# Routing chunk by chunk inside the last output unit, first expert's tokens by slot-matrix products, gates by pair in the last round

## Chip, cores and metric

The kernel runs on one core of one Trainium2 chip. The metric is the device time of one execution in microseconds (us), lower is better. The core's engines are named as the profile names them: PE (matrix products; PEld its weight loads), DVE (vector), ACT (scalar), POOL (GpSimd) and SP, which here only issues DMAs.

## The reference, cut to what matters

One decoder block over 512 tokens of width 1024: a mixer of four retention heads and four dilated attention heads, an output projection added to the input, then a mixture of experts in which each token goes to 4 of 32 experts, and a last RMSNorm. The part around the change:

```python
x = x + hybrid_mixer(rms_norm(x, norm_mix_g[l]), w_in[l], w_out[l], pos)
x = x + moe_ffn(rms_norm(x, norm_ffn_g[l]), ...)
# moe_ffn:
logits = (ht @ w_router + b_router).astype(jnp.float32)
top_val, top_idx = lax.top_k(logits, TOP_K)                     # 4 of 32
gates = jax.nn.softmax(top_val, axis=-1).astype(h.dtype)
...                                                             # tokens sorted by expert, blocks of 128 rows
gu = xb @ w_gu + b_gu                                           # 128 x 1024 by 1024 x 2048
act = min(x_glu, 7) * sigmoid(1.702 * x_glu) * (clip(x_lin, -7, 7) + 1)
y = act @ w_dn + b_dn                                           # 128 x 1024 by 1024 x 1024
out.at[rows_tok].add(y * rows_gate[:, None])
```

## The kernel before

All weights come in units of 1 MB (128 partitions x 2048 numbers). Units 0 to 13 are the input projection, 14 to 17 the output projection (`U_OUT`), and from 18 on (`U_MOE`) each expert has 8 gate and up units and 4 down units. Each unit is loaded by SP into a raw slot, split by ACT into a rounded high part (`hi(n)`, line 693) and by DVE into the remainder (`lo(n)`, line 992), and PE makes three products with it (activation high and low by weight high, activation high by weight low): 12 products of 512 columns a unit. There are four split slots, so `hi(n)` waits until PE has used unit n-4, and six raw slots, so SP loads unit n once `lo(n-6)` is done. Every engine has its program written out by hand, and semaphores carry the order between them. An engine that waits holds up all that stands behind it in its own program.

The 512 tokens are four chunks of 128 (`c` = 0..3). In the last output unit (`out_project(U_OUT + 3, c)`) PE finishes the second half of each chunk's output, DVE adds it to the residual (`residual(1)`, line 1155), POOL multiplies the chunk by the norm's gain (`hn`, line 557), ACT sums its squares (line 805), and PE transposes the halves (line 1603) and multiplies them with the router (line 1613). When all four chunks are there, DVE makes the root, the logits, the four choices and a 0/1 mask for all of them at once (lines 1166 to 1193), PE turns the masks into places in the experts' lists (1638 to 1642), and DVE compares them with slot numbers (`has`, line 1198). PE makes from that the row numbers of expert 0 and 1 (1651), and POOL gathers the rows of expert 0 from memory (line 595), after which PE transposes them (`tokens`, 1663) and ACT and DVE split them. `first_gate_up` then runs expert 0's eight gate and up units (1685, 1687, 1693).

For the other experts a table in memory is used. POOL stores it with 16 indirect DMAs (`store_entries`, line 611), reads it back (`tab`, line 635), and copies a column as the index of each gather. In the main loop, round i runs the gate and up units of expert i+1 (`gate_up`, lines 1722 to 1727), `tokens(2, i)`, which transposes the rows gathered for expert i+2, and the down units of expert i. POOL in a round: two bias rows spread over the partitions (lines 526 and 534), the gather for expert i+3, the scatter of expert i (601, 605). After 30 rounds a tail handles the last two experts, and the biases of the down projection are added as one product of the gates by pair (`gate4`) and all 32 rows.

Before the loop starts, these things stand behind one another on POOL, in this order: the bias spread of expert 0, the gather for expert 0, four entries, a bias spread, four entries, the gather for expert 1, eight entries, the two bias spreads of expert 1 (which `bias_to_gate(1)` on ACT and then the first unit of the loop on PE wait for), the table, the gather for expert 2. DVE makes the gates by pair (1223 to 1231) and the list of overflowing experts (1282 to 1294) before the loop, and ACT waits for that list before `hi(30)`.

Of the kernel before, what the change touches and what calls it, by code (L numbers as in the profile page):

```python
# [25 lines left out]
P = 128  # L26
# [129 lines left out]
def build(nc, x, norm_mix_g, w_in, w_out, norm_ffn_g, w_router, b_router,  # L156
# [77 lines left out]
    pair_gate, o = place(o, "pair_gate", [NC, E])  # L234
    pair_pos, o = place(o, "pair_pos", [NC, E])
    prod, _ = place(area + 70 * K, "prod", [NC * TOPK, E])
    top8, o = place(o, "top8", [NC, 8])
    idx8, o = place(o, "idx8", [NC, 8], U32)
    idxf, o = place(o, "idxf", [NC * TOPK])
# [21 lines left out]
    bias_over, _ = place(area + 12 * K, "bias_over", [2 * D])  # L261
    counts, o = place(area + 20 * K, "counts", [E])
# [11 lines left out]
    x1_at = base + RAW * UNIT * 4 + 2 * SPLIT * UNIT * 4  # L274
    xT0_hi, _ = place(x1_at + 8 * K, "xT0_hi", [KD, P], F32R)
    xT0_lo, _ = place(x1_at + 12 * K, "xT0_lo", [KD, P], F32R)
# [8 lines left out]
    gate4, _ = place(area + 92 * K, "gate4", [NC, 4, E])  # L285
    gateT, o = place(area + 102 * K, "gateT", [S], F32R)
# [35 lines left out]
    pairs_all = sem("pairs_ready")  # L322
    gather_index, scatter_index, order = sem("gather_index"), sem("scatter_index"), sem("gpsimd_order")
    counts_s, total_s = sem("counts_ready"), sem("total_ready")
    sq, var_s, root_s, rstd_s = sem("squares"), sem("variance"), sem("root"), sem("rstd")
# [24 lines left out]
    gate4_s, gate_zero, gate_tr, gateT_hi, gateT_lo = (sem("gates_copied"), sem("gate_rows_cleared"), sem("gates_transposed"),  # L350
# [4 lines left out]
    xg_zero = sem("rows_cleared")  # L355
# [47 lines left out]

    def raw_unit(r, rows):
        return raw_slot(r).rearrange("p (k c) -> p k c", k=rows)
# [15 lines left out]
    with block as block:  # L421
        @block.sync
        def _(sp):
# [19 lines left out]
            def load_bias_rows(e, i):  # L443

                sp.wait_ge(gate_all, i + e)
                sp.dma_start(row_g[0:1, :], b_gate_up[0, bass.ds(i + e, 1), 0:D]).then_inc(bias_in, 16)
                sp.wait_ge(lin_all, i + e)
# [13 lines left out]
            sp.wait_ge(logit_s, 2)  # L461
# [21 lines left out]
            sp.wait_ge(moved, 32 * (E - 2) + 64)  # L483
# [28 lines left out]
        def _(pl):  # L512
# [7 lines left out]
            def spread_gate_bias(e, i=0):  # L520

                pl.wait_ge(bias_in, 16 if e == 0 else i * 32 + 32 * (e + 1))
                if e > 0:
                    pl.wait_ge(bias_gate, i + e)
                    pl.sem_inc(order, 1)
                nc.gpsimd.partition_broadcast(bias_g[:, :], row_g[0:1, :]).then_inc(gate_all, 1)

            def spread_lin_bias(e, i=0):

                pl.wait_ge(bias_in, i * 32 + 32 * (e + 1))  # L530
                if e > 0:
                    pl.wait_ge(bias_lin, i + e)
                    pl.sem_inc(order, 1)
# [25 lines left out]
            pl.wait_ge(logit_s, 2)  # L559
            spread_gate_bias(0)  # L560
            pl.wait_ge(gate_all, 1)
# [1310 lines left out]
```

## Time and profile before

| | us |
|---|---|
| median of 3 runs (1445.2 to 1447.88) | 1445.6 |
| the profiled execution | 1446.0 |
| its span | 1444.2 |
| PE busy | 1387.5 (96%) |
| DVE busy | 1232.4 (85%) |
| ACT busy | 1024.2 (71%) |
| POOL busy | 410.3 (28%) |

Busy time is a share of the whole span. The stretches around the change look different from the average, and a wait counts only if nothing else is late by as much. All instants below are us from the span's start.

### The profile page before, as it was taken

What the parts mean: (1) busy time and instruction counts of PE and PEld (TensorE: products, weight loads), DVE (VectorE), ACT (ScalarE), POOL (GpSimd) and SP (SyncE); (2) the same over time, 40 slices, a digit from 0 to 9 for tenths busy, and PEclk for the clock granted to TensorE, in tenths of its full rate; (3) what the DMA queues carried; (4) which work ended last, traced back from release to release, by engine and by line L of the source; (5) the groups of instructions that cost most, each with busy time, mean ns of one, the idle gap of its engine ahead of it and who ended that gap; (6) DMA issues with size and microseconds to landing.
All of it is one profiled execution on the core that took longest, in us unless ns stands there. A gap on an engine that the chain in (4) does not pass through costs nothing.

```text
span 1444.2 us, 19518 instructions
## 1 busy us (share of the span) xinstructions
PE 1387.5 (96%) x6520; PEld 1153.0 (80%) x6520; DVE 1232.4 (85%) x927; ACT 1024.2 (71%) x750; POOL 410.3 (28%) x231
## 2 busy tenths in 40 slices
PE   6999999877999999999999999999999999999995
PEld 5877888766888888888888888888888888888874
DVE  5534547367999999999999999999999999999986
ACT  5234334465788888888888888888888888888874
POOL 0000001284633333333333333333333333333311
PEclk9999999978999999999999999999999999999998
DMA  8221224456999999999999999999999999999993
GB/s 300 94 82 59 100 76 136 157 211 223 379 396 383 381 384 380 372 374 382 378 382 387 370 382 379 377 382 383 381 376 386 380 386 385 381 385 380 372 338 124
DMA packets 81017, 453.48 MB, mean 314 GB/s; under 512 B 13887, under 2 KB 13903, under 8 KB 32736
## 3 DMA queue, kind: packets, MB, share of 16 engines
q1 hardware_dynamic: 68968, 432.55, 75.6%
q0 software_dynamic: 10304, 18.26, 4.9%
q10 hardware_dynamic: 1720, 2.34, 0.5%
q8 instruction: 16, 0.26, 0.1%
q14 instruction: 9, 0.07, 0.0%
HBM read 447.63 MB, written 22.59 MB: 326 GB/s over the span
## 4 chain that ended last, share of the span: by engine, by line
PE 86%; DMA 4%; DVE 3%; POOL 2%; ACT 2%; issue 2%; ACTq 0%; SPq 0%; DVEq 0%; POOLq 0%
PE ps L1722 14%; PE ps L1727 14%; PE ps L1723 14%; PE ps L1685 8%; PE ps L1687 8%; PE ps L1693 8%; PE ps L1415 4%; PE ps L1423 4%; PE ps L1416 4%; DMA acc_rows<-y,idx_scatter 2%; PE ps L1663 2%; PE ps L1676 2%; ACT whi L693 1%; POOL slot_table L611 1%; POOL idx_scatter L601 1%
## 5 line engine op out<-in xcount | busy, mean ns | idle before, releaser
L992 DVE TENSOR_TENSOR wlo<-raw,whi 128x2048 fp32r<-128x2048 f32 x274 | 648.7, 2390 | 108.0 <-ACT whi L693 107.7
L693 ACT ACTIVATE whi<-raw 128x2048 fp32r<-128x2048 f32 x274 | 520.8, 1914 | 137.2 <-PE ps L1727 91.6
L1722 PE MATMUL ps<-whi,xT_hi 128*128 128x512 f32 x992 | 390.4, 394 | 8.3 <-ACT ps L854 8.3
L1723 PE MATMUL ps<-whi,xT_lo 128*128 128x512 f32 x992 | 387.1, 390 | 0.0
L1727 PE MATMUL ps<-wlo,xT_hi 128*128 128x512 f32 x992 | 266.4, 390 | 0.0
L1722 PEld LDWEIGHTS ps<-whi,xT_hi 128*128 128x128 f32 x992 | 187.0, 189 | 47.0 <-issue 8.7
L1727 PEld LDWEIGHTS ps<-wlo,xT_hi 128*128 128x128 f32 x992 | 186.8, 188 | 38.9
L1723 PEld LDWEIGHTS ps<-whi,xT_lo 128*128 128x128 f32 x992 | 187.1, 189 | 37.9
L1685 PE MATMUL ps<-whi,actT_hi 128*128 128x512 f32 x496 | 195.9, 395 | 0.0
L1687 PE MATMUL ps<-whi,actT_lo 128*128 128x512 f32 x496 | 193.2, 390 | 0.0
L601 POOL COPY idx_scatter<-tab 128x1 uint32 (+1 forms) x31 | 59.0, 1904 | 321.9 <-ACT y L841 321.9
L992 DVE TENSOR_TENSOR wlo<-raw_a,whi 128x2048 fp32r<-128x2048 f32 x64 | 145.9, 2279 | 2.2 <-ACT whi L693 2.0
L992 DVE TENSOR_TENSOR wlo<-raw_b,whi 128x2048 fp32r<-128x2048 f32 x64 | 145.9, 2280 | 1.1 <-ACT whi L693 1.1
L693 ACT ACTIVATE whi<-raw_a 128x2048 fp32r<-128x2048 f32 x64 | 122.8, 1918 | 24.1 <-PE ps L1727 24.1
L693 ACT ACTIVATE whi<-raw_b 128x2048 fp32r<-128x2048 f32 x64 | 122.5, 1915 | 23.9 <-PE ps L1727 23.9
L1693 PE MATMUL ps<-wlo,actT_hi 128*128 128x512 f32 x496 | 132.8, 390 | 0.2 <-DVE wlo L992 0.2
L601 POOL COPY idx_gather<-tab 128x1 uint32 (+1 forms) x31 | 12.6, 406 | 354.7 <-PE ps L1663 353.0
L1693 PEld LDWEIGHTS ps<-wlo,actT_hi 128*128 128x128 f32 x496 | 93.0, 188 | 20.2 <-DVE wlo L992 0.6
L1687 PEld LDWEIGHTS ps<-whi,actT_lo 128*128 128x128 f32 x496 | 93.2, 188 | 18.4
L1685 PEld LDWEIGHTS ps<-whi,actT_hi 128*128 128x128 f32 x496 | 93.2, 188 | 18.4
L534 POOL PARTITION_BROADCAST bias_l<-row_l x32 | 99.5, 3110 | 0.0
L605 POOL DMA_INDIRECT acc_rows<-y,idx_scatter x31 | 87.5, 2824 | 27.4 <-POOL idx_scatter L601 27.4
(229 smaller groups left out, 1648.8 us busy)
## 6 DMA issues: line engine op xcount, KB each, us to landing
raw<-in_w_gate_up SPq DMA_DIRECT2D x130, 1024.0 KB, 8.7
raw<-in_w_down SPq DMA_DIRECT2D x126, 1024.0 KB, 9.4
raw_a<-in_w_gate_up SPq DMA_DIRECT2D x63, 1024.0 KB, 6.8
raw_b<-in_w_gate_up SPq DMA_DIRECT2D x63, 1024.0 KB, 7.3
raw<-in_w_in SPq DMA_DIRECT2D x14, 1024.0 KB, 5.2
raw<-in_w_out SPq DMA_DIRECT2D x4, 1024.0 KB, 5.1
x<-in_x SPq DMA_DIRECT2D x4, 512.0 KB, 8.0
acc_rows<-x SPq DMA_DIRECT2D x4, 512.0 KB, 4.9
```

Source lines behind the costliest of these rows:

```text
L534: nc.gpsimd.partition_broadcast(bias_l[:, :], row_l[0:1, :]).then_inc(lin_all, 1)
L601: return nc.gpsimd.tensor_copy(index[:, 0:1], tab[:, bass.ds(e, 1), 0].bitcast(U32))
L605: pl.indirect_dma_start(out=acc_rows, out_offset=bass.IndirectOffsetOnAxis(ap=idx_scatter[:, 0:1], axis=0), in_=y[:, :], in_offset=None, b ...
L693: nc.scalar.activation(whi_slot(n), raw_slot(slot_of(n)), ACT.Copy).then_inc(hi_done, 1)
L992: nc.vector.tensor_tensor(wlo_slot(n), raw_slot(slot_of(n)), whi_slot(n).bitcast(F32), ALU.subtract).then_inc(lo_done, 1)
L1415: mm(out_ap, x_hi_of(k), w_hi_ap, start=opened and k == 0, stop=False)
L1685: mm(ps[:, bank + half, :], x_hi_t[:, k0 + k, :], w_hi_ap, start=k0 + k == 0 and not started, stop=False, skip_group_check=started)
L1687: mm(ps[:, bank + half, :], x_lo_t[:, k0 + k, :], w_hi_ap, start=False, stop=False, skip_group_check=started)
L1693: last = mm(ps[:, bank + half, :], x_hi_t[:, k0 + k, :], w_lo_ap, start=False, stop=k0 + k == KD - 1, skip_group_check=started)
L1722: mm(ps[:, part, :], xT_hi[:, u, :], w_hi_ap, start=False, stop=False, skip_group_check=True)
L1723: mm(ps[:, part, :], xT_lo[:, u, :], w_hi_ap, start=False, stop=False, skip_group_check=True)
L1727: last = mm(ps[:, part, :], xT_hi[:, u, :], w_lo_ap, start=False, stop=u == U_GU - 1, skip_group_check=True)
```

## The change

Four things move.

1. Routing chunk by chunk. DVE no longer handles all four chunks at once: after each `add_residual(c)` it makes that chunk's variance and inverse root, and `pick(c)` and `give_places(c)` make its choices and places, in an order written out between the residual additions. PE does routing of chunks 0 to 2 and the places of chunk 0 ahead of `out_project(U_OUT + 3, 3)`. ACT takes the squares in halves, with roots and row scaling in between.
2. The first expert's tokens are no longer gathered: PE multiplies the scaled rows with the 0/1 matrix of slots (`first_tokens`, eight fp32 products of 128x128 a chunk), summed over the chunks in two PSUM banks, and ACT and DVE split the two halves apart. Expert 0's biases come by two broadcast DMAs instead of a spread on POOL.
3. The row numbers and the gather for expert 1, and all that belongs to the table, stand behind the start of expert 0: `second_rows` on PE is in front of its third unit, POOL spreads both bias rows of expert 1 ahead of the 16 entries, which it then issues in one run.
4. The gates by pair are made on POOL after the last loop round, and slot matrix and overflow list of the last expert on DVE in the last round (between `lo(38)` and `lo(39)`).

On PE, in the last output unit, the rows of before (`x_52` is the residual, `catT` the concatenated heads; the row `x8` ends the routing of all four chunks):

```order
L1423 MATMUL ps<-wlo,catT_hi 128x512 x4
L1603 MATMUL ps<-cst,x_52 128x128 x4
L1613 MATMUL ps<-wr,rT 128x32 x4
L1603 MATMUL ps<-cst,x_52 128x128 x4
L1613 MATMUL ps<-wr,rT 128x32 x8
L1638 MATMUL ps<-masks,tri_r 128x128
L1640 MATMUL ps<-masks,ones_r 128x96
L1640 MATMUL ps<-masks,ones_r 128x64
L1640 MATMUL ps<-masks,ones_r 128x32
L1642 MATMUL ps<-masks,ones_r 128x32 x4
```

And of the change, from the end of the last chunk's unit to the first unit of expert 0 (`has_148` is the new slot matrix, L1711 is `first_tokens`):

```order
L1494 MATMUL ps<-wlo,catT_hi 128x512 x4
L1700 MATMUL ps<-masks,ones_r 128x32
L1703 MATMUL ps<-masks,tri_r 128x32
L1711 MATMUL ps<-has_148,hn 128x128 x8
L1676 MATMUL ps<-cst,x_52 128x128 x4
L1711 MATMUL ps<-has_148,hn 128x128 x8
L1688 MATMUL ps<-wr,rT 128x32 x4
L1700 MATMUL ps<-masks,ones_r 128x32 x2
L1703 MATMUL ps<-masks,tri_r 128x32
L1711 MATMUL ps<-has_148,hn 128x128 x8
L1700 MATMUL ps<-masks,ones_r 128x32 x3
L1703 MATMUL ps<-masks,tri_r 128x32
```

Ahead of that unit now stand the routing products of chunks 0 to 2 and the mask product of chunk 0, and behind it the slot-matrix products, chunk by chunk, each behind the places of its chunk.

On POOL, between the norm's gain and the loop, the rows of before (L526 and L534 are the spreads of the two bias rows, L595 the gathers, L611 the entries):

```order
L526 ISA bias_g<-row_g 128x1024
L595 DMA xg<-h_rows,idx_first 128x1024
L611 DMA slot_table<-entry,entry_at 4096x2 x4
L534 ISA bias_l<-row_l 128x1024
L611 DMA slot_table<-entry,entry_at 4096x2 x4
L595 DMA xg<-h_rows,idx_first 128x1024
L611 DMA slot_table<-entry,entry_at 4096x2 x8
L526 ISA bias_g<-row_g 128x1024
L534 ISA bias_l<-row_l 128x1024
L635 DMA tab<-slot_table 128x64
L601 COPY idx_gather<-tab 128x1
L595 DMA xg<-h_rows,idx_gather 128x1024
```

And of the change (L539 and L546 are the spreads, L603 the gathers, L619 the entries):

```order
L539 ISA bias_g<-row_g 128x1024
L603 DMA xg<-h_rows,idx_first 128x1024
L546 ISA bias_l<-row_l 128x1024
L630 MEMSET gate_147 128x4x32
L619 DMA slot_table<-entry,entry_at 4096x2 x16
L636 DMA tab<-slot_table 128x64
L609 COPY idx_gather<-tab 128x1
L603 DMA xg<-h_rows,idx_gather 128x1024
```

One gather and one pair of spreads are gone, the spreads of expert 1 stand ahead of the entries, and the 16 entries stand in one run behind them.

On DVE, after the residual addition of the second chunk, the rows of the change (L1205 to L1039 are variance and inverse root, L1218 to L1229 are `pick`):

```order
L1243 TENSOR_TENSOR x_52<-x_52,ps 128x512
L1205 SCALAR_TENSOR_TENSOR small<-small 128x1
L1035 RECIPROCAL small<-small 128x1
L1036 TENSOR_TENSOR small<-small 128x1
L1037 TENSOR_TENSOR small<-small 128x1
L1038 TENSOR_SCALAR small<-small 128x1
L1039 TENSOR_TENSOR small<-small 128x1
L1243 TENSOR_TENSOR x_52<-x_52,ps 128x512
L1218 SCALAR_TENSOR_TENSOR logits<-ps,small,br 128x32
L1220 MAX top_104<-logits 128x8
L1221 MAX_INDEX idx_105<-top_104,logits 128x8
L1222 CAST idxf<-idx_105 128x4
```

Before, the four residual additions stood there in one run, and the variance came once, behind them.

The diff, cut to its core:

```diff
@@ gpsimd
-            pl.wait_ge(logit_s, 2)
-            spread_gate_bias(0)
...
+            spread_gate_bias(1)
             pl.wait_ge(idx_first_s, 1)
             pl.wait_ge(hn_out, 16 * NC)
             gather_rows(idx_first[:, 0:1], moved)
+            spread_lin_bias(1)
+            pl.wait_ge(x_tr, 1)
+            link(nc.gpsimd.memset(gate4[:, :, 3, :], 0.0))
             pl.wait_ge(entry_s, 1)
             pl.wait_ge(table_cleared, 16)
-            for j in range(4):
+            for j in range(NC * TOPK):
                 store_entries(j)
-            spread_lin_bias(0)
-            for j in range(4, 8):
-                store_entries(j)
-            pl.wait_ge(idx_first_s, 2)
-            pl.wait_ge(x_tr, 1)
-            pl.wait_ge(moved, 16)
-            gather_rows(idx_first[:, 1:2], moved)
-            for j in range(8, NC * TOPK):
-                store_entries(j)
-            spread_gate_bias(1)
-            spread_lin_bias(1)
             pl.wait_ge(entry_out, 16 * NC * TOPK)
...
+            pl.wait_ge(chosen_s, 1)
+            link(nc.gpsimd.tensor_tensor(prod2[:, :, :], chosen2[:, :, :],
+                                         entry[:, :, 1].unsqueeze(2).to_broadcast([P, NC * TOPK, E]), ALU.mult))
...
@@ sync
-                sp.wait_ge(gate_all, i + e)
+                sp.wait_ge(gate_all, i + (e - 1))
@@ scalar
+            square_half(1, 0)
+            row_root(0)
+            store_residual(NC)
+            square_half(1, 1)
+            row_root(1)
+            scale_row(0)
...
+            act_e.wait_ge(used, U_MOE)
+            act_e.dma_start(bias_g[:, :], b_gate_up[0, 0:1, 0:D].to_broadcast([P, D])).then_inc(bias0_in, 16)
+            act_e.dma_start(bias_l[:, :], b_gate_up[0, 0:1, D:2 * D].to_broadcast([P, D])).then_inc(bias0_in, 16)
+            store_residual(NC + 3)
+            row_root(3)
+            scale_row(3)
+            hi(20)
...
+            hi(21)
+            first_index()
             bias_to_lin(0)
@@ vector
+            add_residual(0)
+            row_variance(0)
+            row_inverse(0)
+            add_residual(1)
+            row_variance(1)
+            row_inverse(1)
+            add_residual(2)
+            pick(0)
+            row_variance(2)
+            pick(1)
+            row_inverse(2)
+            give_places(0)
+            add_residual(3)
+            give_places(1)
+            pick(2)
+            row_variance(3)
+            row_inverse(3)
+            give_places(2)
+            pick(3)
+            give_places(3)
...
@@ tensor
+                if g and c >= 2:
+                    pe.wait_ge(mask_s, c - 1)
...
+            def first_tokens(c):
+
+                pe.wait_ge(has0_s, c + 1)
+                pe.wait_ge(hn_s, c + 1)
+                for j in range(KD):
+                    last = mm(ps[:, 2 + j // 4, (j % 4) * P:(j % 4 + 1) * P], hn[:, c, j * P:(j + 1) * P], has0[:, c, :],
+                              start=(c == 0 and j % 4 == 0), stop=(c == NC - 1), skip_group_check=True)
...
+            transpose_residual(NC + 2)
+            route(NC + 1)
+            route(NC + 2)
+            positions(0)
+            out_project(U_OUT + 3, 3)
+            positions(1)
+            first_tokens(0)
+            transpose_residual(NC + 3)
+            first_tokens(1)
+            route(NC + 3)
+            positions(2)
+            first_tokens(2)
+            positions(3)
+            first_tokens(3)
```

## Rows read from the trace of the kernel before

**Rows 1.** Stretches: length, busy PE, PEld, DVE, ACT, POOL, granted clock, DMA share, GB/s.

```profile
275.00:300.00 25.00, 13.59 (x82) 12.28 (x79) 16.27 (x54) 13.07 (x18) 13.82 (x13) 0.68 0.56 213
325.00:1400.00 1075.00, 1065.64 (x4930) 887.52 (x4929) 1031.01 (x541) 869.99 (x555) 356.64 (x189) 1.00 0.95 375
```

**Rows 2.** Waits between 336 and 400: us in total, times, longest.

```profile
PE ps L1722 <- ACT ps L854: 8.3, 1, 8.3
PE ps L1663 <- DMA acc_rows<-y,idx_scatter: 0.8, 1, 0.8
```

**Rows 3.** Timeline of PE: start, us, what.

```profile
302.74 0.76 PE L1685 MATMUL ps<-whi,xT_hi 128*128 128x512 f32 x1 [2.59 <-issue]
307.88 0.40 PE L1685 MATMUL ps<-whi,xT_hi 128*128 128x512 f32 x1
...
310.61 0.39 PE L1685 MATMUL ps<-whi,xT_hi 128*128 128x512 f32 x1
...
326.94 1.07 PE L1693 MATMUL ps<-wlo,xT_hi 128*128 128x512 f32 x4
336.29 0.79 PE L1722 MATMUL ps<-whi,xT_hi 128*128 128x512 f32 x1 [8.29 <-ACT ps L854]
...
341.57 0.53 PE L1722 MATMUL ps<-whi,xT_hi 128*128 128x512 f32 x1
```

**Rows 4.** The same at the end of the loop's first eight units.

```profile
361.68 1.03 PE L1663 MATMUL ps<-cst,xg 128*128 128x128 f32 x8
```

**Rows 5.** Timeline of DVE: start, us, what, idle before.

```profile
281.45 1.04 DVE L1166 SCALAR_TENSOR_TENSOR small<-small,cst 128x4 f32<-128x4 f32 x1 [1.41 <-ACT squares L805]
...
283.04 0.16 DVE L998 TENSOR_TENSOR small<-small 128x4 f32<-128x4 f32 x1
...
315.66 2.29 DVE L992 TENSOR_TENSOR wlo<-raw,whi 128x2048 fp32r<-128x2048 f32 x1 [0.55 <-ACT whi L693]
318.26 2.29 DVE L992 TENSOR_TENSOR wlo<-raw,whi 128x2048 fp32r<-128x2048 f32 x1 [0.30 <-ACT whi L693]
...
344.06 0.86 DVE L1288 TENSOR_TENSOR ovr<-ovr,ovf 128x96 f32<-128x96 f32 x1
...
377.20 8.89 DVE L992 TENSOR_TENSOR wlo<-raw,whi 128x2048 fp32r<-128x2048 f32 x4
```

**Rows 6.** Timeline of POOL over the same time.

```profile
270.51 4.78 POOL L557 TENSOR_TENSOR hn<-x,g_row 128x1024 f32<-128x1024 f32 x2 [25.20 <-DVE x L1155]
...
280.11 2.36 POOL L557 TENSOR_TENSOR hn<-x,g_row 128x1024 f32<-128x1024 f32 x1 [1.67 <-DVE x L1155]
...
316.31 2.51 POOL L611 DMA_INDIRECT slot_table<-entry,entry_at  x1 [0.30 <-issue]
...
332.52 0.98 POOL L611 DMA_INDIRECT slot_table<-entry,entry_at  x1 [0.30 <-issue]
...
335.99 0.64 POOL L635 DMA_DIRECT2D tab<-slot_table  x1
338.28 0.18 POOL L601 COPY idx_gather<-tab 128x1 uint32<-128x1 uint32 x1 [1.65 <-DMA tab<-slot_table]
339.36 3.04 POOL L595 DMA_INDIRECT xg<-h_rows,idx_gather  x1 [0.90 <-POOL idx_gather L601]
...
343.65 1.30 POOL L534 PARTITION_BROADCAST bias_l<-row_l  x1
...
376.24 9.89 POOL L601 COPY idx_scatter<-tab 128x1 uint32 x1 [9.17 <-ACT y L841]
```

**Rows 7.** All 16 entries: ns min/median/max, first and last start; their landing.

```profile
L611 POOL DMA_INDIRECT slot_table<-entry,entry_at x16: 982/1726/3088, 295.1 to 332.5; - x16
DMA to landing us min/median/max: 2.2/4.2/7.9
```

**Rows 8.** The chain that ended last: start, us, what.

```profile
293.58 4.55 DMA xg<-h_rows,idx_first
```

**Rows 9.** Timeline of DVE in the tail.

```profile
1409.31 1.22 DVE L1260 TENSOR_TENSOR xT_lo<-ps,xT_hi 128x1024 fp32r<-128x1024 f32 x1
```

More of the change, by code:

```diff
@@ L800, in _ @@
             hi(19)
-            for c in range(NC):
-                act_e.wait_ge(x1_s, NC + c + 1)
-                if c:
-                    act_e.wait_ge(sq, NC + c)
-                nc.scalar.activation(squares[:, :], x1[:, c, :], ACT.Square,
-                                     accum_out=small[:, 0, c:c + 1]).then_inc(sq, 1)
-                store_residual(NC + c)
-            act_e.wait_ge(var_s, 2)
-            nc.scalar.activation(small[:, 2, 0:NC], small[:, 1, 0:NC], ACT.Sqrt).then_inc(root_s, 1)
@@ L889, in _ @@
             hi(29)
-            act_e.wait_ge(ov_num, 1)
-            with nc.allow_non_contiguous_dma(reason="16 pairs of numbers onto one partition"):
-                for k in range(2):
-                    act_e.dma_start(ov_lists[0:1, k, :], ov_int[0:16, k:k + 1]).then_inc(ov_s, 16)
             with act_e.Fori(0, E - 2) as i:
@@ L926, in _ @@
                 hi(n, i)
-            gated_rows(E - 2, 32 * (E - 2) + 48, U_ALL - U_DN)
+            gated_rows(E - 2, 32 * (E - 2) + 32, U_ALL - U_DN)
             hi(41, i)
+            act_e.wait_ge(ov_num, 1)
+            with nc.allow_non_contiguous_dma(reason="16 pairs of numbers onto one partition"):
+                for k in range(2):
+                    act_e.dma_start(ov_lists[0:1, k, :], ov_int[0:16, k:k + 1]).then_inc(ov_s, 16)
             act_e.wait_ge(gate_tr, 1)
@@ L1170, in _ @@
-            inverse_root(small[:, 1, 0:NC], small[:, 2, 0:NC], small[:, 3, 0:NC], small[:, 13, 0:NC])
-            v.sem_inc(rstd_s, 1)
-            v.wait_ge(logit_s, 2)
-            flat = logits[:, :, :].rearrange("p c e -> p (c e)")
-            link(nc.vector.tensor_tensor(flat, flat, ps[:, 7, 0:NC * E], ALU.add))
-            for c in range(NC):
-                last = nc.vector.scalar_tensor_tensor(out=logits[:, c, :], in0=logits[:, c, :],
-                                                      scalar=small[:, 3, c:c + 1], in1=br[:, :], op0=ALU.mult, op1=ALU.add)
@@ L1263, in features_lo @@
                                         ALU.subtract).then_inc(aT_lo, 1)
-            tokens_lo(0, 0, xT0_hi, xT0_lo)
-            v.wait_ge(hn_gain, NC)
-            for n in (21, 22, 23, 24, 25, 26):
+            for n in (22, 23, 24, 25, 26):
                 lo(n)
@@ L1638, in _ @@
[L1638 to L1649 removed]
+            out_project(U_OUT + 3, 0)
```

360 lines of the change are left out of this document (205 added, 155 removed).

## The prediction

> **What bounds the kernel now.** I read the stretches first. Behind 325 PE is busy for 1065.64 of 1075 us at the full clock [rows 1]: the loop is PE's own work, and a gain ahead of the loop is kept to the end if nothing else is late where PE arrives. The place to look at is the start of the experts: from 275 to 300 PE is busy 13.59 of 25 us at a mean clock of 0.68, so one of its two levels, 2.4 GHz, is lost to 1.2 for a good part [rows 1]. The waits behind it name one large item, 8.3 us of the loop's first product behind ACT's bias copy, which was itself behind POOL [rows 2], and a small one, 0.8 us behind the first scatter. PE's timeline gives the instants: expert 0 starts at 302.74 and its first unit takes 5.14 us against 2.73 for the next (cold clock, 2.4 lost); its last unit ends about 328.0; the loop starts at 336.29, again cold (5.28 for the unit, 2.6 lost) [rows 3]; its eight units end with `tokens(2)` at 361.68 [rows 4]. All later work follows from that instant, so I forecast it.
>
> Last, DVE and POOL beside each other show that they shut each other out. DVE's variance, a tiny operation, takes 1.04 us and ends with POOL's gain product (282.49 and 282.47); a 128x96 product takes 0.86 us and ends with POOL's spread (344.92 and 344.95) [rows 5, 6]. The other way, an entry issued in a `lo` takes 2.51 us and ends 0.87 behind it, while one without a `lo` takes 0.98; and a POOL copy begun in a run of `lo`s without gaps between them took 9.89 us and ended with the run (386.13 against 386.09) [rows 5, 6]. The entries are POOL work that will lie in the densest `lo`s.
>
> **The change, step by step.**
>
> *Routing.* Chunk 0 is added to the residual by 270.4, where POOL's gain product starts [rows 6]; now half-width squares ahead of `hi(19)` push that by 0.6, to 271.0. Its square needs 0.8, then the variance finds POOL in the gain product (2.36 to 2.4 us [rows 6]) and waits 1.7; 0.2 for the root, five linked operations at 0.2 (0.16 and the gap [rows 5]) for the inverse, 0.7 for the next addition. That is 4.5 us a chunk, so chunk 1 is added at 275.5 and chunk 2 at 280.0. `pick(0)` (8 instructions, about 1.7) is held at its two-input comparison by the third gain product until 282.5, its mask stands at 283.3, and 1.1 of small products later, at 284.4, PE may start the last chunk's unit, which ended at about 279.3 before (0.7 for the addition ahead of 280.11 [rows 6]). PE was mostly idle for 7 us, so I charge it the cold unit of [rows 3], 5.1: 289.5. From there: addition 0.7, gain product 2.4, rest of `pick(2)` 0.8, variance to inverse 1.5, `give_places(2)` 0.7, `pick(3)` 1.7, last places 1.2, half of the last eight fp32 products 0.9, high and low halves 1.4: 300.9. Expert 0 starts there, 1.8 us earlier than 302.74, and with a warm clock (2.4 more). Bounds: 296.5 if neither lock nor clock holds; 305 if the slot-matrix products run at 1.2 GHz too.
>
> *Expert 0.* Eight units at 2.73, 1.0 for `second_rows`, 0.8 for `tokens(1)`: PE is through at 324.5. The spreads of expert 1 are ahead of the entries, so the 8.3 us wait goes. What is late next is DVE: `sigmoid(0)` puts its `lo(26)` end at 322.2, and the gate product, `lo(27)`, `tokens_lo(1)`, `lo(28)`, the clamp and ACT's bias copy (1.1, 2.2, 1.2, 2.2, 1.1, 1.2; a full-width DVE operation is 1.22, [rows 9]) give the loop's third product at 331.2. The rest of the unit 1.8, seven units 19.1, `features` 0.8: PE is ready for `tokens(2)` at 352.9, 8.8 us earlier than 361.68.
>
> *The table.* The entries began at 295.1 [rows 7]. Now they need the shares, which DVE makes behind `lo(21)`, and POOL reaches them behind `bias_to_lin(0)`, which ACT reaches behind `first_index`, that is behind PE's second unit: 310.3. `lo(22)` starts at the same moment and ACT is ahead, so `lo(22)` to `lo(25)` run without a gap: the first entry takes 9.6. Before, the last seven took from 316.31 to 333.50, 2.46 each with the pauses [rows 6]; twelve more at that rate take 29.5, to 349.4, and three when DVE has run dry (0.98 + 0.30) 3.8: 353.2. No spread covers the landing any more (2.2 at the least [rows 7]): 1.5. Then the table's way back 2.3, the index copy and 0.9, and a gather of 4.55 [rows 6, 8]: **362.6**. Bounds for the 16 entries: 20.5 us if no `lo` holds them (0.98 + 0.30 each), 46 if each of them meets a `lo` and the first the whole run; by the nearest rows, the dense seven, I take 42.9.
>
> So `tokens(2)` moves from 361.7 to 362.6: +0.9. PE has then stood for 10 us and restarts cold, which at 336.29 cost 2.6 [rows 3]: +2.6. The 0.8 wait for the first scatter goes, since DVE no longer works off a backlog in that round: -0.8.
>
> *The tail.* Slot matrix and overflow list put 0.9 and 3.9 us of DVE between `lo(38)` and `lo(39)`. `features_lo` stood at 1409.31 [rows 9]; with both, `lo(39)` ends at 1417.5 where PE wants it at 1417.7, and `lo(40)`, `lo(41)` come in time as well: 0, and up to +1.5 if I am 1 us short. The gates by pair, six or so POOL operations, have the 30 us between POOL's last two scatters: 0. The last scatter's index copy no longer starts in a run of `lo`s, which may bring the rows back earlier: -0.5.
>
> The sum on the profiled execution: 1446.0 + 0.9 + 2.6 - 0.8 - 0.5 = 1448.2. That execution is 0.4 above the median, so **1447.8**, slower by 0.15%. (0.2%, 2.9 us, is about what a measurement of this kernel tells from no change.)
>
> The lock on the variance is the step with the thinnest evidence, one row of 1.04 us and one of 0.86 [rows 5]. With it expert 0 starts at 300.9; without it (twice 1.7, and 0.8 in `pick(0)`) at about 297, and the sum is 1444. The Trainium skill (SBUF — State Buffer, Who interferes with whom) says that a DVE instruction with two SBUF inputs contends with a GpSimd instruction that reads SBUF, and that the later one is blocked until the first is through; on these two rows it agrees, and by it the first sum stands.
>
> **The rivals.**
>
> *The entries do not hold PE.* All 16 took 34 us without the foreign work between them (295.1 to 333.5 [rows 7], less a gather of 3.04 and a spread of 1.30 [rows 6]), 2.1 each. At 2.1 they end at 344.4 and the rows are there at 353.8, 0.9 behind PE. The sum is then 1446.0 - 7.9 - 0.8 - 0.5 = 1436.8, and this rival's time 1437. It decides if the entries end by 343. Against it: the first entries, not the last seven, make that mean low, and DVE ran no `lo`s for much of them. The same page states that `tensor_tensor` takes only the read side of the pair while descriptor generation needs the write side (it calls that inferred); by it the entries would take 20.5 us and this rival would hold, but the 2.51 of [rows 6] speaks against it here.
>
> *Late start, slower.* The one mechanism is PE's clock in the broken routing: if the gaps between small products keep it at 1.2 GHz through the slot-matrix products, each group of eight takes 3.6 instead of 1.8, three of them are on the chain, and expert 0 starts at 305. Entries and table shift with it, by 4.1: 1452. It decides once expert 0 starts later than 302. For it: a mean of 0.68 over 25 us is 9 us at full clock and 16 at half [rows 1], so the clock had fallen by about 284, soon after the last unit's end. Against it: PE has more to do in that stretch than it had.
>
> **How the numbers follow.** Forecast 0.58, its own range 1444 to 1451.5 (start of expert 0 and entry rate each worth 3 to 4 us); entries not binding 0.24; late start 0.18. Faster by over 0.2%: 0.24 + 0.03 = 0.27. Within: 0.33. Slower: 0.22 + 0.18 = 0.40. The range takes in the bulk of both rivals: 1436 to 1453.
>
> **What the changed profile would show.** The second and third residual additions near 275 and 280 and variances that end with a gain product; the last chunk's unit starting near 284; expert 0 at 301; no wait behind the spreads; 16 entries from 310 to 353, the first one very long; PE waiting some 10 us for the gather in front of `tokens(2)`, and a clock of 0.5 behind it. If that wait is missing, the first rival holds. If entries do not lengthen with `lo`, my step on the lock is wrong; if PE waits in the tail between units 39 and 41, the tail is.

## The result, and the profile after

The change made the kernel slower: 1455.6 us median of 4 runs (1452.94 to 1458.88) against 1445.76 (1445.2 to 1447.88), ratio 1.0067, 95% interval 1.0056 to 1.0079. The forecast was 1447.8 with a range of 1436 to 1453: slower by over 0.2% had a chance of 0.40, faster 0.27, and the size lies outside the range. The profiled execution is the fastest of the four: 1452.94, span 1451.2 against 1444.2. Of all executions of the experiments below one, of `e5`, is left out of its ratio: it took 2370.1 us at a mean granted clock of 0.56, against 0.99 for the five others, and nothing here explains it.

First the stretches, columns as in [rows 1], after the change:

```profile
280.00:285.00 5.00, 4.17 (x20) 4.06 (x20) 4.55 (x17) 2.56 (x5) 2.36 (x1) 0.50 0.26 105
290.00:300.00 10.00, 7.90 (x67) 7.46 (x67) 7.80 (x29) 5.03 (x7) 3.93 (x5) 1.00 0.86 278
...
318.00:364.00 46.00, 35.10 (x147) 27.75 (x145) 37.32 (x20) 27.50 (x18) 30.19 (x20) 0.92 0.96 338
364.00:375.00 11.00, 6.25 (x21) 5.34 (x22) 3.19 (x3) 4.24 (x4) 4.76 (x5) 0.55 0.25 81
```

The clock was at its lower level (1.2 GHz, 0.50) from 280 to 285, after PE had been idle for 3.08 us ahead of 280.13, and back at 2.4 GHz for the slot-matrix products (1.00 from 290). It fell again at about 364, with PE idle since 358.5. The new fact is the DMA share of 0.96 from 318 to 364. Before, the same stretch of the program had a hole in it; two stretches of the kernel before:

```profile
318.00:328.00 10.00, 10.00 (x49) 8.02 (x47) 7.89 (x5) 8.97 (x7) 8.78 (x5) 1.00 0.92 343
328.00:338.00 10.00, 1.71 (x5) 1.42 (x5) 5.72 (x5) 2.84 (x3) 8.01 (x6) 0.68 0.03 5
```

PE's timeline after the change, the instants of [rows 3, 4]:

```profile
302.93 0.47 PE L1789 MATMUL ps<-whi,xT_hi 128*128 128x512 f32 x1 [0.56 <-issue]
320.98 1.09 PE L1767 MATMUL ps<-cst,xg 128*128 128x128 f32 x8 [0.55 <-DMA xg<-h_rows,idx_first]
329.22 0.49 PE L1830 MATMUL ps<-whi,xT_hi 128*128 128x512 f32 x1 [1.67 <-DVE xT_lo L1323]
333.61 0.80 PE L1830 MATMUL ps<-whi,xT_hi 128*128 128x512 f32 x1 [3.21 <-issue]
368.75 1.97 PE L1767 MATMUL ps<-cst,xg 128*128 128x128 f32 x8 [10.22 <-DMA xg<-h_rows,idx_gather]
```

Expert 0 starts when it did, but warm. The wait of 8.3 us for the bias is down to 1.67 and 3.21. Behind these two the clock is at 0.50 once more, from 334 to 338. PE is through with the loop's eight units at 358.5 (368.75 less 10.22) and then stands 10.22 us for the rows of expert 2: `tokens(2)` is at 368.75, where it was at 361.68. From there to the high half of the last output (`y_hi`, 1432.34 now, 1424.27 before) the two kernels differ by 1.0 us more, and the tail gives 1.07 back: 7.07 + 1.0 - 1.07 = 7.0, the whole difference of the spans.

POOL's timeline says what the rows wait for, the entries abridged:

```profile
311.05 1.30 POOL L539 PARTITION_BROADCAST bias_g<-row_g  x1 [13.95 <-ACT ps L900]
312.55 3.34 POOL L603 DMA_INDIRECT xg<-h_rows,idx_first  x1 [0.20 <-issue]
315.95 2.19 POOL L546 PARTITION_BROADCAST bias_l<-row_l  x1
...
319.12 1.95 POOL L619 DMA_INDIRECT slot_table<-entry,entry_at  x1 [0.83 <-POOL gate L630]
321.37 1.84 POOL L619 DMA_INDIRECT slot_table<-entry,entry_at  x1 [0.30 <-issue]
...
350.38 2.42 POOL L619 DMA_INDIRECT slot_table<-entry,entry_at  x1 [0.30 <-issue]
357.64 0.61 POOL L636 DMA_DIRECT2D tab<-slot_table  x1 [4.84 <-DMA slot_table<-entry,entry_at]
363.21 0.19 POOL L609 COPY idx_gather<-tab 128x1 uint32<-128x1 uint32 x1 [4.97 <-DMA tab<-slot_table]
364.29 1.07 POOL L603 DMA_INDIRECT xg<-h_rows,idx_gather  x1 [0.89 <-POOL idx_gather L609]
```

The 16 entries run from 319.12 to 352.80, POOL then waits 4.84 us for the last of them to land, the table needs 5.57 from its issue to the index copy (2.29 before, [rows 6]), and the gather 4.46. From the end of the last entry to `tokens(2)` are 15.95 us. What fills the DMA queues meanwhile is SP, which issues the weight loads; its rows:

```profile
323.04 0.31 SPq L460 DMA_DIRECT2D row_g<-in_b_gate_up  x1
323.56 0.23 SPq L462 DMA_DIRECT2D row_l<-in_b_gate_up  x1
325.11 0.37 SPq L446 DMA_DIRECT2D raw_a<-in_w_gate_up  x1
...
354.82 22.05 SPq L446 DMA_DIRECT2D raw<-in_w_gate_up  x4
```

Before, the same bias rows went out at 335.15, behind the gate spread of expert 1:

```profile
333.51 1.47 POOL L526 PARTITION_BROADCAST bias_g<-row_g  x1
335.15 0.30 SPq L446 DMA_DIRECT2D row_g<-in_b_gate_up  x1
```

SP waits for that spread before it overwrites the row, and the spreads stood behind the entries. All weight loads behind the bias rows in SP's program were held with them; that is the hole of 0.03, and the last entry (issued at 332.52) and the table landed in it. With the spreads ahead, SP runs on at 323.

### The profile page after: what moved, and what is told of

It reads as the page before. It is cut to its first block, busy times and chain, and to the rows that moved or that the text cites. A ratio compares the mean times of both kernels' runs of the same rounds, so it can differ in the third digit from the quotient of the medians.

```text
span 1451.2 us, 19737 instructions
## 1 busy us (share of the span) xinstructions
PE 1396.0 (96%) x6578; PEld 1159.8 (80%) x6578; DVE 1245.2 (86%) x957; ACT 1026.4 (71%) x761; POOL 395.9 (27%) x236
## 4 chain that ended last, share of the span: by engine, by line
PE 88%; DVE 3%; DMA 3%; POOL 2%; ACT 2%; issue 2%; ACTq 0%; DVEq 0%; POOLq 0%
PE ps L1830 15%; PE ps L1835 15%; PE ps L1831 15%; PE ps L1789 8%; PE ps L1791 8%; PE ps L1797 8%; PE ps L1486 4%; PE ps L1487 4%; PE ps L1494 4%; PE ps L1767 2%; PE ps L1780 2%; POOL slot_table L619 1%; DVE wlo L1030 1%; DMA gmix<-in_norm_mix_g 1%; DMA acc_rows<-y,idx_scatter 1%
## 5 line engine op out<-in xcount | busy, mean ns | idle before, releaser
L609 POOL COPY idx_scatter<-tab 128x1 uint32 (+1 forms) x31 | 44.0, 1420 | 307.9 <-ACT y L881 307.9
L546 POOL PARTITION_BROADCAST bias_l<-row_l x31 | 99.2, 3200 | 0.1
L613 POOL DMA_INDIRECT acc_rows<-y,idx_scatter x31 | 91.5, 2951 | 27.4 <-POOL idx_scatter L609 27.4
```

Of the source, the lines that this page charges most:

```text
L546: nc.gpsimd.partition_broadcast(bias_l[:, :], row_l[0:1, :]).then_inc(lin_all, 1)
L613: pl.indirect_dma_start(out=acc_rows, out_offset=bass.IndirectOffsetOnAxis(ap=idx_scatter[:, 0:1], axis=0), in_=y[:, :], in_offset=None, b ...
```

## The experiments

Each ran beside the kernel before on the same chip; ratios are to that kernel, which took 1445.1 to 1445.6 there. Differences between two versions are differences of their medians.

**1. Is it the table?** Rows of expert 2 without the table (the third slot matrix goes through `second_rows` and `first_index` like that of expert 1):

```diff
@@ vector
+            slots_of(has, num, lambda c: pair_pos[:, c, 2:3])
...
@@ gpsimd
-            for j in range(NC * TOPK):
+            for j in range(8):
                 store_entries(j)
+            pl.wait_ge(x_tr, 2)
+            pl.wait_ge(moved, 16)
+            gather_rows(idx_first[:, 1:2], moved)
+            for j in range(8, NC * TOPK):
                store_entries(j)
...
-            table_index(idx_gather, 2).then_inc(gather_index, 1)
...
-            gather_rows(idx_gather[:, 0:1], moved)
```

> The second looped expert's row indices (expert 2) come from a slot-matrix product of their own, as expert 1's do, instead of from the slot table; its gather stands between entries 8 and 9 of the POOL queue; everything else is the change as it is. Theory 'table chain' (in the changed kernel PE stood 10.2 us from 358.5 for the rows of expert 2, because the last entry, its landing, the table's way back and the gather follow each other): that wait goes, the cold restart behind it (about 2 us) goes too, and the time falls from 1455.6 to 1443 (1440 to 1447), below the kernel before. Rival 'weight stream' (the DMA queue of weights sets the loop, so a wait at its start is only taken back later): within 2 us of 1455. Rival 'next wait': the bias rows of expert 2 or the scatter of expert 0, which still need the table, stop PE instead: 1448 to 1453.

Measured: 1448.1 us (10 runs, 1444.8 to 1451.7), ratio 1.0013 [1.0002, 1.0024]. The wait of 10.2 is gone from the trace and 7.5 of the 9.8 us that the change had lost with it, so the rival that the weight stream takes it back is out. The first theory's range ended at 1447, 1.1 us below. The rest is new waits, so the time stands at the lower edge of the third theory: PE in the same places as above,

```profile
324.91 1.97 PE L1771 MATMUL ps<-cst,xg 128*128 128x128 f32 x8 [3.42 <-DMA xg<-h_rows,idx_first]
...
376.10 0.50 PE L1834 MATMUL ps<-whi,xT_hi 128*128 128x512 f32 x1 [2.60 <-ACT whi L707]
```

the second one a split behind ACT's bias copy of expert 2, whose spread stands behind the table on POOL.

**2. What does an entry cost, and where is it landed?** Eight entries more, ahead of the others, into a memory table that nobody reads:

```diff
+            for j in range(8):
+                store_entries(j, spare_table)
             for j in range(NC * TOPK):
                 store_entries(j)
-            pl.wait_ge(entry_out, 16 * NC * TOPK)
+            pl.wait_ge(entry_out, 16 * (NC * TOPK + 8))
```

> The change as it is, with 8 entries more ahead of the 16, written into a table that nobody reads. Theory 'table chain': every entry stands on the path of PE one for one, so the time rises by 8 times 1.3 to 2.4 us: +10 to +19, to 1466 to 1475. Rival 'landing alone' (the DMAs' landing behind the weight loads is what counts; the entries' own issue could be hidden): below +5.

Measured: 1463.0 us (4 runs), ratio 1.0123 [1.0107, 1.0140], 7.4 above the change: between the two theories, and below the range of the first. The trace tells why:

```profile
369.31 0.61 POOL L639 DMA_DIRECT2D tab<-slot_table  x1 [1.47 <-DMA slot_table<-entry,entry_at]
371.54 0.19 POOL L610 COPY idx_gather<-tab 128x1 uint32<-128x1 uint32 x1 [1.63 <-DMA tab<-slot_table]
```

The last entry ended at 367.84 (366.86 and 0.98), 15.0 us later than in the change, all of it on PE's path. But PE had stopped by then, nobody used up split slots, and the weight loads stopped too (mean DMA share 0.30 from 362 to 377). So the landing cost 1.47 instead of 4.84 and the table 2.23 instead of 5.57, and 6.7 us of the 15.0 came back: `tokens(2)` at 376.92, 8.2 later.

**3. The landing by itself.** SP is held after a round's loads until the table is in:

```diff
                 load_round(i, True)
+                sp.wait_ge(tab_in, 16)
```

> The change, with SP held after the first looped expert's weight loads until the slot table is back in SBUF, so that the three loads at 349.4, 352.1 and 354.8 us do not stand in the DMA queues beside the last entries and the table. Theory 'landing': the last entry lands in 2 to 3 us instead of 4.8 of waiting, the table comes back in 2.2 to 2.5 instead of 5.5, rows of expert 2 reach PE about 5 us earlier (near 363.7 instead of 368.75); time 1450 (1448 to 1453) if the held loads are not missed later, 1455 to 1458 if the stream of weights is what bounds the next expert. Rival 'POOL alone': landing times do not change, 1455.6 within 1 us.

Measured: 1455.0 us (4 runs), ratio 1.0063 [1.0046, 1.0080], no different from the change. Its POOL and PE rows:

```profile
315.21 1.30 POOL L540 PARTITION_BROADCAST bias_g<-row_g  x1 [17.25 <-issue]
...
356.29 0.60 POOL L637 DMA_DIRECT2D tab<-slot_table  x1 [1.46 <-DMA slot_table<-entry,entry_at]
358.38 1.08 POOL L610 COPY idx_gather<-tab 128x1 uint32<-128x1 uint32 x1 [1.49 <-DMA tab<-slot_table]
360.36 2.71 POOL L604 DMA_INDIRECT xg<-h_rows,idx_gather  x1 [0.89 <-POOL idx_gather L610]
```
```profile
370.35 1.97 PE L1768 MATMUL ps<-cst,xg 128*128 128x128 f32 x8 [9.78 <-DMA xg<-h_rows,idx_gather]
```

Both landings fell as the landing theory says (1.46 and 1.49 of waiting), so the rival "POOL alone" is out. But the held loads were let go at 359.0 to 362.6, on both sides of the gather's issue at 360.36, and the gather took 9.95 us to land instead of 4.4: `tokens(2)` at 370.35, where the theory had 363.7. My "missed later" was the wrong place for the loss; the total is right for another reason. The wait moved from the table to the gather.

This run also says something on why the change's median lies 2.7 us above its profiled execution. Up to the held loads the two programs are the same, yet the spread of expert 1 began at 315.21 instead of 311.05 and PE waited 3.37 instead of 0.55 for the rows of expert 1. The first difference is PE's last output unit; its last products in the change, then here:

```profile
288.77 1.09 PE L1494 MATMUL ps<-wlo,catT_hi 128*128 128x512 f32 x4
288.85 1.88 PE L1495 MATMUL ps<-wlo,catT_hi 128*128 128x512 f32 x4
```

In the change's profiled execution the granted clock rose from 0.50 between 288 and 289 (mean 0.73) and the unit took 4.29 us; here it was still 0.50 at 290 and the unit took 5.26, and expert 0 started at 303.79 instead of 302.93. The second difference is the landing of the four stores of scaled rows in memory (7.6/9.3/10.1 us at least/median/most; 5.9/8.7/9.6 in the profiled execution), which ACT waits for before it issues the bias row (306.0 against 303.5).

**4. POOL's gain product beside the routing.** The version of 1, with gain and scale of a chunk's rows in one DVE operation; then the same on the change itself:

```diff
-                nc.gpsimd.tensor_tensor(hn[:, c, :], x1[:, c, :], g_row[:, :], ALU.mult).then_inc(hn_gain, 1)
...
-                nc.scalar.activation(hn[:, c, :], hn[:, c, :], ACT.Copy, scale=small[:, 3, c:c + 1]).then_inc(hn_s, 1)
...
+                nc.vector.scalar_tensor_tensor(out=hn[:, c, :], in0=x1[:, c, :], scalar=small[:, 3, c:c + 1],
+                                               in1=g_row[:, :], op0=ALU.mult, op1=ALU.mult).then_inc(hn_s, 1)
```

> The third-rows version of the same call, and the gain and scale of the rows (POOL product of 2.35 us and ACT scale of 1.15 us for each chunk) in one DVE operation of about 1.2 us for each chunk, right behind the chunk's inverse root, so that no POOL product runs beside the DVE's routing. Theory 'shared port' (DVE operations stood until the POOL product ended: 1.70, 1.65, 1.75 and 2.38 us instead of 0.2 to 0.3): these fall to their plain lengths, the last chunk's path loses the 2.35 of POOL and gains about 1.2 of DVE, and the first expert starts 1 to 3 us earlier than 302.9; 1 to 3 us below the third-rows version. Rival 'DVE's queue': the four operations of 1.2 us push the choices of each chunk back by as much, and the time is the same as the third-rows version or 1 to 2 us above.

> The change as it is, table chain and all, with the gain and scale of the rows in one DVE operation for each chunk. Theory 'table chain': the entries' arithmetic comes about 1 to 2 us earlier and so do the entries, the table and the rows of expert 2: time 1455.6 less 1 to 2, 1453.5 to 1454.5. Rival: the landing of the rows of h and of the bias row sets the entries' start, and the time does not move (1455 to 1456).

Measured: 1445.4 on top of 1 (ratio 1.0000 [0.9990, 1.0009]), 1452.6 on the change (1.0052 [1.0035, 1.0069]): 2.7 and 3.0 us less by the medians. Each of the two intervals still touches that of the version without the edit, and the profiled executions differ by nothing and by 1.7. The first rows are DVE after the change, the next that of the version on top of 1:

```profile
271.71 1.70 DVE L1205 SCALAR_TENSOR_TENSOR small<-small 128x1 f32<-128x1 f32 x1 [0.79 <-ACT squares L818]
276.32 1.65 DVE L1205 SCALAR_TENSOR_TENSOR small<-small 128x1 f32<-128x1 f32 x1 [0.79 <-ACT squares L818]
280.79 1.75 DVE L1222 CAST idxf<-idx 128x4 f32<-128x4 uint32 x1
290.73 2.38 DVE L1237 TENSOR_SCALAR has<-num,pair_pos 128x128 f32<-128x128 f32 x1
```
```profile
271.67 0.16 DVE L1200 SCALAR_TENSOR_TENSOR small<-small 128x1 f32<-128x1 f32 x1 [0.79 <-ACT squares L814]
```

Without a POOL product beside it the variance takes 0.16 instead of 1.70 and 1.65. On the change expert 0 then started at 299.8 instead of 302.93, but the entries at 318.8 instead of 319.12, because the first spread (next experiments) began at 310.87 all the same. The prediction's step on the lock stands. Its price is at most the 3 us, since the edit also takes POOL's 2.35 and ACT's 1.15 us out of each chunk's path.

**5. Two new orders on POOL that failed.** `e7` is the change with the gather of expert 1 ahead of its gate spread. `e5` is version 1 with gather, two entries, the two spreads, the rest, and the wait for the table behind the spreads of expert 2; `e6` is `e5` with the rows on DVE.

```diff
+            pl.wait_ge(hn_out, 16 * NC)
+            pl.wait_ge(idx_first_s, 1)
+            gather_rows(idx_first[:, 0:1], moved)
             spread_gate_bias(1)
-            pl.wait_ge(idx_first_s, 1)
-            pl.wait_ge(hn_out, 16 * NC)
-            gather_rows(idx_first[:, 0:1], moved)
```

> The change as it is, but the gather of expert 1 ahead of the spread of its gate bias row in the POOL queue, so that it no longer waits for a bias row to land. PE's wait for expert 1's rows (0.5 us in the profiled run, 3.4 in slower ones) goes. Theory 'table chain': PE waits for the table of expert 2 anyway and the entries start when they did, so the time stays within 1 us of 1455.6. Rival 'first gather': the time falls by 2 to 3 us, to about 1453.

> The third-rows version with the POOL queue put in another order and nothing else: the gather of expert 1 first, then two entries, the two spreads of expert 1's bias rows, the other entries; and the wait for the slot table behind the spreads of expert 2's bias rows instead of ahead of them. In the third-rows version PE stood 3.4 us for the rows of expert 1 (gather issued at 317.0, behind a spread that waited for its bias row) and 2.6 us at 376.1 for a weight split queued on ACT behind the bias of expert 2 (spread at 368.8 to 372.1, after the table). Theory 'next waits': both go, and the time falls from 1448.1 by 4 to 6 us, to 1442 to 1444. Rival 'weight stream': the second wait is of weights that land late anyway, and only 0 to 3 us come, 1445 to 1448.

> The same, with gain and scale of the rows in one DVE operation for each chunk, as in the run on rows on DVE. There the first expert started 301.7 instead of 302.9 to 303.5 and the median fell from 1448.1 to 1445.4. Theory: its 1.5 to 2.5 us add to what the moved spreads bring, 1440 to 1442. Rival: with both waits gone the loads of weights are what PE waits for, and the time is that of the moved spreads alone within 0.7.

Measured: 1458.2 (1.0085 [1.0069, 1.0102]), 1450.8 (1449.8 for the five executions that the ratio uses; 1.0036 [1.0023, 1.0050]) and 1448.0 (1.0018 [1.0008, 1.0027]). `e7` and `e5` were slower than both of my theories allowed. `e6` missed its 1440 to 1442 as well, though the rows on DVE brought their share again, 2.8 us below `e5`, where the rival had them bring at most 0.7. First `e7`, then `e5`:

```profile
311.60 1.14 POOL L603 DMA_INDIRECT xg<-h_rows,idx_first  x1 [13.12 <-ACT idx_first L887]
320.23 3.36 POOL L539 PARTITION_BROADCAST bias_g<-row_g  x1 [7.49 <-issue]
```
```profile
327.94 1.30 POOL L539 PARTITION_BROADCAST bias_g<-row_g  x1 [10.13 <-issue]
```

The spread begins 7.49 and 10.13 us after POOL was free, though its bias row had gone out at 306.4 and 303.2. In `e7` the entries began at 327.76 instead of 319.12 and `tokens(2)` at 373.64; in `e5` PE stood 3.6 us for the bias, and 4.4 for a weight split at 374.56. These misses raised a new question: what does the first broadcast of a program wait for?

**6. The first broadcast.** One small broadcast into an array that nobody reads any more, while POOL is idle: on the change (`e9`), on `e6` (`e10`), and on the version of 4 (`e11`).

```diff
+            pl.wait_ge(hThi_s, KD)
+            pl.wait_ge(hTlo_s, KD)
+            link(nc.gpsimd.partition_broadcast(gmix[:, :], cst[0:1, 0:KD]))
```

> The change as it is, with one small partition broadcast (8 constants over an array of gains that nobody reads any more) added on POOL at about 250 us, where POOL is idle. In every run so far the first partition broadcast of the program began 6 to 10 us after POOL had reached it and its semaphores were there: before, 288.9 after 282.5 (nobody waited); the change, 311.05 with its last bias row issued at 303.5; gather first, 320.2 after 312.7; spreads moved, 327.9 after 317.8; later broadcasts begin at once. Theory 'first call': the early broadcast takes this on itself, the spread of expert 1 starts about 305 instead of 311, the gather of expert 1 at 309.3 to 310 instead of 312.5 to 317, the entries at 313 to 314 instead of 319 to 323, and the table chain ends 5 to 8 us earlier: 1447 to 1451. Rival 'bias row': the spread waits for its row to land; then nothing moves, 1455.6 within 1.

> Third rows, spreads moved and rows on DVE (1448.0) with the same early broadcast. Its spreads began at 325.1, 10.2 us after POOL was free at 314.9, and PE stood 3.6 us for the bias at 327.7 and 4.3 at 370.8. Theory 'first call': the spreads begin at once, the first wait goes, the entries and the table come 8 to 10 us earlier, the second wait goes too: 1440 to 1443, below both kernels. Rival 'bias row' or 'weight stream': 1446 to 1448.

> Third rows and rows on DVE in the order of the change (1445.4), with the early broadcast. PE stood 3.4 us for the rows of expert 1 and 3.1 at 372.3 for a weight split behind the bias of expert 2. Theory 'first call': the gather of expert 1 comes 5 us earlier and so do the entries and the table, both waits go, 1439 to 1442. Rival: 1445 to 1446.

Measured: 1455.0 (1.0062 [1.0046, 1.0079]), 1446.1 (1.0001 [0.9991, 1.0010]) and 1440.1 (0.9955 [0.9939, 0.9972]): no gain, 2 us, and 5.3 us. By time alone only `e11` (1439 to 1442) came out as the theory said; `e9` and `e10` fell into the ranges of their rivals, so the rows have to decide. Two rows of `e9`, then one of `e11` and one of `e10`:

```profile
254.14 0.59 POOL L569 PARTITION_BROADCAST gmix<-cst  x1 [8.81 <-issue]
...
312.13 1.30 POOL L539 PARTITION_BROADCAST bias_g<-row_g  x1 [13.94 <-ACT ps L903]
```
```profile
303.01 1.42 POOL L539 PARTITION_BROADCAST bias_g<-row_g  x1 [9.17 <-DMA row_l<-in_b_gate_up]
```
```profile
316.73 2.48 POOL L539 PARTITION_BROADCAST bias_g<-row_g  x1
```

The early broadcast began 8.81 us after POOL was free, and it waits for no DMA, and its two semaphores are those of `hT`, whose last write ends at 20.6 us. The spread of `e11` then began 1.6 us after its bias row was issued (301.41), and that of `e10` at once behind two entries, where it had been 10 us late: the first call has a price, and it is not the row. The Trainium skill (GPSIMD Engine Reference, Instruction dispatch) states that the first call of a freshly loaded kernel pays for loading its code, about 6 us, with no visible instruction. The traces agree that no instruction shows, and have more than that figure: 8.18, 8.52, 8.78 and 8.81 us in the four runs where the early broadcast stands alone (`e10`, `e11`, `e12` of the next experiment, `e9`). Before, the price was hidden: POOL stood 6.46 ahead of 288.93 while the routing was still under way.

But on the change itself the early broadcast buys nothing: in `e9` the spread still began at 312.13, 7.6 us after its row was issued at 304.52, and some 6.7 after the row had landed (the two packets of its DMA queue ran at about 305.4). Two causes offer themselves. One is that POOL found no gap to enter, since DVE ran from 304.74 to 313.66 with no gap of more than 0.2, and its operation beside the spread took 1.13 instead of 0.18. `e10` speaks against it: there the spread began at 316.73 in the middle of four `lo` that DVE ran in one piece from 311.35 to 321.22. The other is that the first call's price came back: in `e9` the four gain products still run on POOL between the early broadcast and the spread, and in the three runs that gained (`e10`, `e11`, `e12`) they do not. No run isolates it, so it stays open.

**7. Is the new order a loss?** The kernel before with the spreads of expert 1 between entries 12 and 13, and nothing else; and `e11` with the spreads of expert 2 right behind the last entry.

```diff
-            for j in range(8, NC * TOPK):
+            for j in range(8, 12):
                 store_entries(j)
             spread_gate_bias(1)
             spread_lin_bias(1)
+            for j in range(12, NC * TOPK):
+                store_entries(j)
```

> The kernel before, with the two spreads of expert 1's bias rows between entries 12 and 13 instead of behind entry 16, and nothing else. There PE stood 8.3 us at 328 for this bias [the one wait that the order of the change is to take away]. The table would come 2.5 us later, near 341 back in SBUF, its rows for expert 2 by 346, and PE would want them from about 354. Theory 'order alone': the bias wait shrinks to 0 to 3 us and the restart is warmer, nothing is given back, 1445.2 falls by 5 to 8 us, to 1437 to 1440: the order is worth what the whole change was to bring, and the loss of the change comes from starting its 16 entries 24 us later. Rival 'weight stream': SP's loads then run beside the entries, landing grows as in the changed kernel (4.8 for the last entry, 5.5 for the table), but PE is reached by neither; the same numbers. Rival 'given back': the wait only moves to the table or to ACT, and the time stays within 2 us of 1445.

> Third rows, rows on DVE, early broadcast (1440.1), and the spreads of expert 2's bias rows right behind the last entry instead of behind the table. There PE stood 2.6 us at 369.0 for a weight split that queued on ACT behind the bias of expert 2 (spread at 360.6 to 365.1). Theory 'table chain': with the spreads at 349 to 353 the wait goes and the time falls by 2 to 3 us, to 1437 to 1438. Rival 'weight stream': the weights of the second round land too late for more than 1 us to come, 1439 to 1440.

Measured: 1441.5 (0.9973 [0.9961, 0.9985]) and 1437.6 (0.9949 [0.9936, 0.9963]). One move in the old kernel gains 4.2 us, less than the 5 to 8 expected. Its rows:

```profile
341.70 0.61 POOL L637 DMA_DIRECT2D tab<-slot_table  x1 [5.16 <-DMA slot_table<-entry,entry_at]
344.09 0.18 POOL L601 COPY idx_gather<-tab 128x1 uint32<-128x1 uint32 x1 [1.78 <-DMA tab<-slot_table]
```
```profile
329.80 0.49 PE L1724 MATMUL ps<-whi,xT_hi 128*128 128x512 f32 x1 [1.36 <-DVE xT_lo L1255]
334.20 0.79 PE L1724 MATMUL ps<-whi,xT_hi 128*128 128x512 f32 x1 [3.21 <-ACT ps L862]
```

The last entry lands as late as in the changed kernel (5.16, at a DMA share of 1.0 from 336 to 342), as expected with SP let go; the table came back in 2.39, not 5.5, in a lull of the loads (0.43 from 342 to 344). Nobody minds, because the table is back at 344, well ahead of PE. The wait of 8.3 shrank to 1.36 and 3.21; the second of them, DVE's clamp and ACT's bias copy, is what I had not counted in the 5 to 8. So spreads ahead of the last entries are a gain. That the late start of the entries spends it in the change follows from these times; no run has the change's order with an early start. `e12` shows no wait of PE between 335 and 400, fell by 2.5 as expected, and is faster than both kernels; its interval overlaps that of `e11`, so the last 2.5 us rest on the medians and on the missing wait.

## Why the prediction was off

*Right.* The chain of the routing (additions near 275 and 280 at 274.84 and 279.38, variances blocked until the gain product ends, the cold last unit from 285.4), the wait for the spreads that goes, no wait in the tail, and PE restarting cold at `tokens(2)`. Expert 0 at 302.93 was inside the bounds of 296.5 to 305, 2 us behind the 300.9: a comparison beside the last gain product was held too (2.38), which I had not charged. The rival of the late clock did not happen: the slot-matrix products ran at the upper level, 2.05 us for 16.

*Wrong, and cancelling.* Entries from 310.3 to 353.2 became 319.12 to 352.80; that the end fits is luck. The start was 9 us late: the spread at 311.05, some 6.6 us after its row had landed (its packets ran at about 304.4), a wait that the sum had at nothing, then the gather's 3.34 and the other spread's 2.19. And the 42.9 us were 33.7. The first entry did not wait for the run of `lo`s, it took 1.95; entries inside the run took about 1.9, beside single `lo`s up to 3.03, and 0.98 with DVE free. At 2.1 an entry this is the rate of the first rival (whose own working takes off the 3.04 of a later gather instead of 2.78, without effect); the late start and the landings kept PE waiting. Without any lengthening beside DVE the 16 would have taken 20.5. The Trainium skill (SBUF — State Buffer, Who interferes with whom) infers that `tensor_tensor` takes only the read side of the shared pair and descriptor generation the write side; the 33.7 measured here speaks against it.

The wait of PE fits by luck as well. 9.7 us were forecast and 10.22 came, but PE was ready at 358.5 and not at 352.9: the product that the sum had at 331.2 came at 333.61, behind the wait of 3.21, and the rest of the eight units took 3.2 more, with the clock at 0.50 from 334 to 338 where the sum had it warm. It cost nothing, because the table was later still.

*The step that failed* is "No spread covers the landing any more (2.2 at the least [rows 7]): 1.5. Then the table's way back 2.3". Measured 4.84 and 5.57, 6.6 us more than the 3.8 charged; `tokens(2)` at 368.75 instead of 362.6 is this term, less 0.4 for the entries' end. For the landing I took the least of [rows 7], whose median was 4.2 and whose most 7.9, and for the table the one row of [rows 6], where the queues were empty, without asking why they were. They were empty because SP waited for spreads that the change moves ahead of the entries. Experiments 2, 3 and 7 show the dependence from both sides (1.47 and 1.46 us of waiting with the loads stopped, 4.84 in the change and 5.16 in `e13` with them running). I had followed the moved spreads to ACT and PE, who wait for them, but not to SP.

*Small terms.* Cold clock and scatter wait together +1.8 predicted, +1.0 measured; tail -0.5 predicted, -1.07 measured. On the profiled execution 1448.2 was forecast and 1452.94 came: +6.1 up to `tokens(2)`, -0.8, -0.6. The other 2.7 us to the median no trace of the change shows, since the profile is of its fastest execution. Five other runs have the same routing (`e1`, `e2`, `e3`, `e7`, `e9`). In four of them the last output unit took 5.03 to 5.27 us instead of 4.29, as the clock rose later (`e2`: 4.33), and in `e1`, `e3` and `e7` the quickest store of the rows of h took 7.4 us or more to land instead of 5.9. So this clock and these landings are likely causes, not shown ones.

## What to carry to other kernels

A wait that goes may also have held a DMA queue: when a producer moves ahead, list everyone who waits for it, SP too, and price small DMAs at what they cost with the loads running (here 4.84 and 5.57 us instead of 1.5 and 2.3). A move that frees the critical engine pays only if the chain behind the moved work still ends before that engine arrives; the old kernel with this one move gained 4 us, the whole change, where the entries start 24 us later, lost 9.8.

## What was not expected of the hardware

- The first partition broadcast of a program began 8.2 to 8.8 us after POOL had reached it (7.5 in `e7` and 10.1 in `e5`, amid other work). Later ones began at once, but for the one of `e9`, some 6.7 us after its row had landed, behind four products on POOL. Placed in an idle stretch the first one cost nothing (1455.0 against 1455.6).
- A POOL product with two inputs also held up DVE operations with one input: a cast (1.75 us instead of 0.17) and a comparison with a scalar (2.38 instead of 0.29), both until the product ended (to 0.1 us).
- A gather issued amid five freshly released loads of 1 MB landed after 9.95 us (`e3`), with the queues freer (DMA share 0.5) after 4.4 in the change.
